# State-space stage: 96 weight units spread evenly over the rounds, outputs ahead of the lag products, x on all partitions

## The reference

```python
sh1, sc1, gt1, sh2, sc2, gt2 = adaln(c, w_mod[layer], b_mod[layer])  # split(silu(c) @ w + b, 6)
csh1, csc1, cgt1, csh2, csc2, cgt2 = adaln(c_ctx, w_mod[layer], b_mod[layer])
h_lat = modulate(rmsnorm(x_lat, norm_mix_pre[layer]), sh1[:, None], sc1[:, None])
h_ctx = modulate(rmsnorm(x_ctx, norm_mix_pre[layer]), csh1, csc1)
# s5_mixer: 128 groups of 16 features, 64 complex states each, for direction in range(2):
    st_ctx = s5_scan(uc_ctx, lam_bar, b_bar, s0, reverse)
    st_lat = s5_scan(uc_lat, lam_bar, b_bar, s_ctx_final, reverse)
    y_lat = y_lat + jnp.einsum('btgp,ghp->btgh', st_lat, c_mat).real
z = jax.nn.gelu(y.reshape(h.shape).astype(h.dtype))
a, g = jnp.split(z @ w_glu, 2, axis=-1)
```

## Time and profile before

| | us |
|---|---|
| median of 3 runs | 3558.69 (3556.96 to 3559.35) |
| the profiled execution, its own time | 3554.54 |
| its span | 3552.7 |
| state-space stage, up to the first GLU matmul | 465.07 |
| TensorE busy over the span | 3286.0 (92%) |
| VectorE, ScalarE, POOL busy | 2145.0, 1380.7, 480.5 |

### The profile page before, as it was taken

One profiled execution on the slowest core, in us unless ns is written; L12 is line 12 of the kernel. 1 busy time (PEld: TensorE's weight loads), 2 busy tenths in 40 slices (PEclk: granted clock), 3 DMA queues, 4 the chain that ended last, 5 costly groups with the idle time before them and its releaser, 6 DMA issues.

```text
span 3552.7 us, 51801 instructions
## 1 busy us (share of the span) xinstructions
PE 3286.0 (92%) x21097; PEld 2763.3 (78%) x21097; DVE 2145.0 (60%) x1850; ACT 1380.7 (39%) x1385; POOL 480.5 (14%) x352
## 2 busy tenths in 40 slices
PE   5788899799999999886789999999999899999998
PEld 3445578688888888675678888888868788888887
DVE  7668755565555555699565555555644555555555
ACT  4446543433333333322234434433323344344332
POOL 2869900000000000096000000000000000000000
PEclk7888899899999999998799999999999999999999
DMA  9988875255555555344145555555524455555552
GB/s 299 305 282 257 260 243 175 91 184 189 185 189 182 190 186 189 107 142 148 36 154 178 186 190 182 186 189 189 177 92 142 142 186 184 187 187 189 189 183 89
DMA packets 351014, 643.22 MB, mean 181 GB/s; under 512 B 21599, under 2 KB 50359, under 8 KB 350519
## 3 DMA queue, kind: packets, MB, share of 16 engines
q1 hardware_dynamic: 309952, 561.68, 48.9%
q10 hardware_dynamic: 40951, 79.98, 6.6%
HBM read 637.54 MB, written 4.06 MB: 181 GB/s over the span
## 4 chain that ended last, share of the span: by engine, by line
PE 83%; DVE 6%; POOL 5%; issue 2%; DMA 2%; ACT 1%; SPq 1%; DVEq 1%; ACTq 0%; POOLq 0%
PE acc L439 49%; PE acc L440 25%; POOL cpow L1841 3%; DMA raw<-in_w_mod_dram 2%; POOL ptmp L1841 1%; PE acc L1263 1%; DVE z L943 1%; DVE w_lo L793 1%; PE acc L1280 1%; PE acc L521 1%; PE acc L533 1%; PE acc L464 1%; PE acc L1188 1%; PE acc L1247 1%; DVE hf L832 0%
## 5 line engine op out<-in xcount | busy, mean ns | idle before, releaser
L439 PE MATMUL acc<-xin,w_hi 128*128 128x512 f32 x5376 | 1915.2, 399 | 58.9 <-DVE xin L807 33.7
L793 DVE TENSOR_TENSOR w_lo<-raw,w_hi 128x2048 fp32r<-128x2048 f32 x484 | 1111.2, 2301 | 1079.0 <-ACT w_hi L640 1078.8
L440 PE MATMUL acc<-xin,w_lo 128*128 128x256 f32 x5376 | 1519.4, 283 | 0.0
L640 ACT ACTIVATE w_hi<-raw 128x2048 fp32r<-128x2048 f32 x484 | 926.8, 1917 | 1365.1 <-PE acc L440 1365.0
L439 PEld LDWEIGHTS acc<-xin,w_hi 128*128 128x128 f32 x5376 | 1017.2, 189 | 312.5 <-issue 35.6
L440 PEld LDWEIGHTS acc<-xin,w_lo 128*128 128x128 f32 x5376 | 1021.5, 190 | 0.0
L439 PE MATMUL acc<-hid,w_hi 128*128 128x512 f32 x2432 | 845.4, 392 | 0.0
L440 PE MATMUL acc<-hid,w_lo 128*128 128x256 f32 x2432 | 681.2, 280 | 0.0
L439 PEld LDWEIGHTS acc<-hid,w_hi 128*128 128x128 f32 x2432 | 455.1, 187 | 101.4
L440 PEld LDWEIGHTS acc<-hid,w_lo 128*128 128x128 f32 x2432 | 459.6, 189 | 0.0
L799 DVE TENSOR_REDUCE tmp<-acc 128x1024 f32<-128x2048 f32 x116 | 265.0, 2284 | 19.9 <-PE acc L440 19.9
(11 more groups left out here) (241 smaller groups left out, 2063.5 us busy)
## 6 DMA issues: line engine op xcount, KB each, us to landing
raw<-in_ffn_w_gate_dram SPq DMA_DIRECT2D x88, 1024.0 KB, 5.2
raw<-in_ffn_w_up_dram SPq DMA_DIRECT2D x88, 1024.0 KB, 5.1
raw<-in_ffn_w_down_dram SPq DMA_DIRECT2D x88, 1024.0 KB, 5.1
raw<-in_w_mod_dram ACTq DMA_DIRECT2D x76, 1024.0 KB, 9.7
raw<-in_w_mlp_in_dram SPq DMA_DIRECT2D x64, 1024.0 KB, 5.2
raw<-in_w_mlp_out_dram SPq DMA_DIRECT2D x64, 1024.0 KB, 5.1
raw<-in_s_w_glu_dram SPq DMA_DIRECT2D x32, 1024.0 KB, 5.3
raw<-in_ab_w_in_dram SPq DMA_DIRECT2D x32, 1024.0 KB, 5.3
```

Of the source, the lines that this page charges most:

```text
L439: pe.matmul(bank, w_hi[:, slot, w], operand[:, kt, :], start=(kt == 0), stop=False)
L440: ins = pe.matmul(bank[:, 0:TOK], w_lo[:, slot, w], operand[:, kt, 0:TOK], start=False, stop=(kt == UK * units - 1))
L640: act.activation(w_hi[:, slot, :], raw[:, slot, :, :].rearrange("p k n -> p (k n)"), ACT.Copy).then_inc(hi_ready, 1)
L793: dve.tensor_tensor(w_lo[:, slot, :], raw[:, slot, :, :].rearrange("p k n -> p (k n)"), w_hi[:, slot, :].bitcast(F32), SUB).then_inc(lo_re ...
```

## The change

Three things. First, weights: `UNIT_OF` lists all 96 units in one order. The first 16 (parts 0 and 1 of MOD) have the old shape, 512 rows by 512 columns in pieces of 2 KB. The other 80 have 256 rows by 1024 columns, so that a piece of a row is 4 KB; they serve two blocks at once. Eight are multiplied ahead of the rounds, then 5 and 6 in turn per round (`FIRST_UNIT`). ScalarE issues them at three places of a round (`ada_load`). Modulation parts 1, 2, 3 are turned at rounds 1, 5, 7.

Second, order: in round k `outputs(k)` now stands ahead of `lag_blocks(k + 1)` and `states(k + 1)`. Lag products go to the lower half of bank 7, so they wait for the copies of the round before (`r_sb`) and `finish` instead of `copy_lam_powers` and `copy_e`. `output_transposes` waits for `r_sb`. VectorE copies the lags inside `powers_of_b`, between its ninth and tenth operation.

Third, x: xs holds all 128 partitions by 4 tokens, loaded in one step; four squares instead of eight, their sums in ss_x, and eight small products with the identity that bring them to the layout of rstd_x.

```diff
-        xs = Region(xin_at, xin_at + 32 * KB)("xs", [64, L // 2, D])
+        xs = Region(xin_at, xin_at + 32 * KB)("xs", [P, L // 2, D])
...
+        xwide = [v.rearrange("(q j) d -> q j d", j=2) for v in (ctx2, x2)]
...
-        MOD = [(0, 1), (2, 3), (6, 8), (10, 12)]
-        ADA = [4, 5, 7, 9, 11] + list(range(13, 24))
-        BLOCK_COL = {MOD[b][v]: (1 - v) * D + b * UN for b in range(4) for v in range(2)}
-        BLOCK_COL.update({m: 2 * D + n * UN for n, m in enumerate(ADA)})
-
-        def ada_units(queue, m, units=range(UK)):
-            col = BLOCK_COL[m]
-            for k in units:
-                if m:
-                    queue.wait_ge(ada_unit, 4 * m + (k - 3))
-                queue.dma_start(raw[:, k, :, :], w_mod[:, k * UK:(k + 1) * UK, col:col + UN]).then_inc(raw_ready[k], 16)
+        def mod_block(b, v):
+            return (1 - v) * D + b * UN, 47 - (16 + 4 * b + 2 * v)
+
+        def ada_block(n):
+            return 2 * D + n * UN, 15 - n
+
+        SINGLE = [mod_block(b, v) for b in range(2) for v in range(2)]
+        PAIRS = [(mod_block(2, v), mod_block(3, v)) for v in range(2)] + [(ada_block(n), ada_block(n + 1)) for n in range(0, KT, 2)]
+        UNIT_OF = [(col, (window,) * 4, [4 * k, 4 * k + 1, 4 * k + 2, 4 * k + 3]) for col, window in SINGLE for k in range(4)]
+        UNIT_OF += [(p[0][0], (p[0][1], p[1][1]) * 2, [2 * j, 2 * j, 2 * j + 1, 2 * j + 1]) for p in PAIRS for j in range(8)]
+        COLUMNS_AT = {1: 1, 5: 2, 7: 3}
+        FIRST_UNIT = [8 + 11 * (r // 2) + 5 * (r % 2) for r in range(KT + 1)]
+        assert FIRST_UNIT[KT] == len(UNIT_OF) == ADA_UNITS
+
+        def ada_load(queue, first, last):
+            for i in range(first, min(last, ADA_UNITS)):
+                slot = i % SLOTS
+                col, _, k = UNIT_OF[i]
+                if i >= SLOTS:
+                    queue.wait_ge(ada_unit, i - 3)
+                if i < 4 * len(SINGLE):
+                    queue.dma_start(raw[:, slot, :, :], w_mod[:, k[0]:k[0] + 4, col:col + UN]).then_inc(raw_ready[slot], 16)
+                else:
+                    queue.dma_start(raw[:, slot, :, :].rearrange("p (k h) n -> p k (h n)", h=2),
+                                    w_mod[:, k[0]:k[0] + 2, col:col + 2 * UN]).then_inc(raw_ready[slot], 16)
...
-            def load_xs(half):
+            def load_xs():
                 for s in range(2):
-                    sp.dma_start(xs[s * NCH:(s + 1) * NCH, :, :], xch[s][:, 4 * half:4 * half + 4, :]).then_inc(xs_in, 16)
+                    sp.dma_start(xs[:, 2 * s:2 * s + 2, :], xwide[s]).then_inc(xs_in, 16)
...
-            load_xs(0)
-            ada_units(sp, 0)
             load_c(0)
+            load_xs()
+            ada_load(sp, 0, 4)
             load_x(0)
-            sp.wait_ge(xs_sq, 4)
-            load_xs(1)
-            ada_units(sp, 1)
-            ada_units(sp, 2)
+            ada_load(sp, 4, 8)
             sp.wait_ge(c_sel, 1)
             load_c(1)
-            ada_units(sp, 3)
             sp.wait_ge(xt_scaled, 1)
             load_x(1)
+            ada_load(sp, 8, 12)
             sp.wait_ge(c_sel, 2)
             load_c(2)
-            ada_units(sp, 4)
             sp.wait_ge(xt_scaled, 2)
             load_x(2)
...
+            def ada_rows(first, last):
+
+                for i in range(first, last):
+                    slot = i % SLOTS
+                    _, window, k = UNIT_OF[i]
+                    pe.wait_ge(raw_ready[slot], 16 * (i // SLOTS + 1))
                     for q in range(UK):
-                        ins = pe.matmul(ps[0][32 * q:32 * q + 32, :], cond[:, kk * UK + q, window:window + 32], raw[:, kk, q, :],
-                                        start=(m + kk == 0), stop=(kk == UK - 1), skip_group_check=True)
+                        ins = pe.matmul(ps[0][32 * q:32 * q + 32, :], cond[:, k[q], window[q]:window[q] + 32], raw[:, slot, q, :],
+                                        start=(i == 0), stop=(i % 4 == 3), skip_group_check=True)
...
-                pe.wait_ge(lpp_sb, min(n + 2, KT))
-                pe.wait_ge(e_sb, 4 * (n + 1))
+                if n == 0:
+                    pe.wait_ge(par_sb, 1)
+                else:
+                    pe.wait_ge(r_sb, n)
+                if n > 1:
+                    pe.wait_ge(z_lo, n - 1)
...
-                            ins = pe.matmul(ps[5][32 * kp:32 * kp + 32, to:to + P],
+                            ins = pe.matmul(ps[7][32 * kp:32 * kp + 32, to:to + P],
...
+                pe.wait_ge(r_sb, min(n + 2, KT))
...
+            pe.wait_ge(b_sb, 3)
+            select_c(0)
+            pe.wait_ge(xs_sq, 4)
+            pe.wait_ge(angle_ready, 1)
+            for f in range(4):
+                for q in range(2):
+                    ins = pe.matmul(ps[2][32 * q:32 * q + 32, 2 * f:2 * f + 2], ident[:, f:P:4], ss_x[:, 2 * q:2 * q + 2], start=True, stop=True)
+            ins.then_inc(ss_tr, 1)
+            ada_rows(0, 8)
...
             for k in range(-1, KT):
-                if k + 1 < KT:
-                    lag_blocks(k + 1, (k + 1) % 2)
-                    states(k + 1, (k + 1) % 2)
+                if k in COLUMNS_AT:
+                    mod_columns(COLUMNS_AT[k])
                 if k >= 0:
                     outputs(k, k % 2)
+                    if k + 1 < KT:
+                        lag_blocks(k + 1, (k + 1) % 2)
                 if k + 1 < KT:
-                    if k in (-1, 2, 4):
-                        pe.wait_ge(ada_sb, {-1: 2, 2: 3, 4: 4}[k])
-                    ada_rows(ADA[k + 1], 15 - (k + 1), (0, 1))
-                if k in (-1, 2, 4):
-                    mod_columns({-1: 1, 2: 2, 4: 3}[k])
+                    states(k + 1, (k + 1) % 2)
+                    if k < 0:
+                        lag_blocks(0, 0)
+                    i0, i1 = FIRST_UNIT[k + 1], FIRST_UNIT[k + 2]
+                if k in COLUMNS_AT:
+                    pe.wait_ge(mod_raw, COLUMNS_AT[k] + 1)
+                if k + 1 < KT:
+                    if k in COLUMNS_AT:
+                        pe.wait_ge(ada_sb, COLUMNS_AT[k] + 1)
+                    ada_rows(i0, i0 + 2)
...
-                    ada_rows(ADA[k + 1], 15 - (k + 1), (2, 3))
+                    ada_rows(i0 + 2, i0 + 4)
                 if k + 2 < KT:
                     transpose_e(k + 2, 1)
-                if 0 <= k < 4:
-                    mod_rows(2 + k // 2, k % 2)
+                if k + 1 < KT:
+                    ada_rows(i0 + 4, i1)
...
-            square_x(0)
             copy_b(2)
             copy_b(3)
+            square_x()
...
-                    ada_units(act, ADA[k + 1] + 1, (0, 1))
+                    i = FIRST_UNIT[k + 1]
+                    ada_load(act, i + 4, i + 6)
                 if k >= 0:
                     copy_output(k)
                 if k + 2 < KT:
                     copy_e(k + 2)
-                    ada_units(act, ADA[k + 1] + 1, (2, 3))
+                    ada_load(act, i + 6, i + 8)
                 if k + 3 < KT:
                     copy_lam_powers(k + 3)
                     normalise_x(k + 3)
-                if 0 <= k < 4:
-                    ada_units(act, ADA[k + 1] + 2)
-                if k in (1, 3):
-                    copy_adarow(2 + k // 2, MOD[2 + k // 2][1])
+                if k + 2 < KT:
+                    ada_load(act, i + 8, FIRST_UNIT[k + 2] + 4)
                 if k == KT - 2:
-                    copy_adarow(4, ADA[KT - 1])
+                    ada_load(act, FIRST_UNIT[k + 1] + 4, FIRST_UNIT[k + 2])
+                if k + 1 in COLUMNS_AT:
+                    copy_adarow(COLUMNS_AT[k + 1], FIRST_UNIT[k + 2])
+                if k == KT - 2:
+                    copy_adarow(4, FIRST_UNIT[KT])
...
+                if between is not None:
+                    between()
                 c(tt(t, pw[1][1], bv[1][0], MUL))
...
+            dve.wait_ge(ss_tr, 1)
+            dve.tensor_scalar(rstd_x[:, :], ps[2][0:64, 0:L], 1.0 / D, EPS, MUL, ADD).then_inc(ss_ready, 1)
             powers_of_b(c0, 0)
-            dve.wait_ge(xs_sq, 8)
-            dve.tensor_scalar(rstd_x[:, :], rstd_x[:, :], 1.0 / D, EPS, MUL, ADD).then_inc(ss_ready, 1)
-            powers([ab[:, 2], ab[:, 3]], uu, L)
             dve.wait_ge(rstd_root, 1)
             dve.reciprocal(rstd_x[:, :], rstd_x[:, :]).then_inc(rstd_ready, 1)
             modulation(cm, 0)
+            powers([ab[:, 2], ab[:, 3]], uu, L)
...
-                if k + 1 < KT:
-                    copy_lags(c0, k + 1)
                 if k:
                     finish(k - 1)
-                if k in (0, 3, 5):
-                    modulation(cm, {0: 1, 3: 2, 5: 3}[k])
                 if k + 2 < KT:
                     dve.wait_ge(s_done, k + 1)
-                    powers_of_b(c0, k + 2)
+                    powers_of_b(c0, k + 2, lambda: copy_lags(c0, k + 1))
+                elif k + 1 < KT:
+                    copy_lags(c0, k + 1)
+                if k in COLUMNS_AT:
```

(1 more changed line is left out.)

49 lines of the change are left out of this document (19 added, 30 removed).

## The result

The changed kernel takes 3575.89 us in the median of 5 runs (3574.53 to 3580.66), the kernel before 3558.69 beside it (3556.96 to 3559.41): 1.005 times as long, with an interval of 1.0038 to 1.0063. The profiled execution took 3574.53 us with a span of 3572.7, against 3554.54 and 3552.7: 20.0 us more. The forecast was 3534.

| stretch | before | after | difference | forecast |
|---|---|---|---|---|
| start, to the lag product of n=2 | 139.56 | 130.65 | -8.9 | -9.5 |
| 13 rounds | 297.2 (22.86 each) | 306.3 (23.56 each) | +9.1 | -16.4 |
| end, to the first GLU matmul | 28.3 | 31.0 | +2.7 | +1 |
| all behind the stage | | | +17.1 | 0 |

What follows compares the result with a forecast made beforehand. Only the state-space stage's 465 us could move, its rounds held by weight loads or POOL's cpow ring. Start -9.5, rounds -16.4, end +1 sum to -24.9 us: 3558.7 becomes 3534 us, range 3510 to 3558.

Steps and rivals of the forecast that it cites:

- Part 1, the start: Up to the third lag product: x loaded whole and fewer units ahead bring the tables earlier, -9.5 us.
- Part 2, the rounds: The 13 rounds between third and sixteenth lag product: 21.6 us each instead of 22.86, -16.4 us.
- DMA sum of 21.1: In each round: the DMA engines' work with evenly spread units, 22.1 us, or 21.1 at a full share of 1.05.
- two rings: In the rounds: DMA work, 21.1 us, and the Toeplitz path from lag product through r, tw, outputs, nearest to 21.8 us.
- 21.8 with tw beside units: In the rounds: the Toeplitz path's length if tw lands beside weight units; 17.4 us at best, 25.5 with both delays.
- columns ahead of outputs: In three rounds: modulation columns turned on TensorE before outputs, a few tenths three times, counted as nothing.
- Rival (d): In the rounds: heavy ones do not wait for weights, so spreading moves nothing; chance left in Rival (b)'s share.
- Rival (b): In the rounds: the Toeplitz path takes both delays, r and tw, 25.5 us a round, 3584 us; chance 0.07.
- TensorE's waits for POOL: In the rounds: outputs no longer wait for cpow, giving 0.8 to 1.6 us against light rounds; POOL's work is 19.3 us.
- Part 3, the end: From the sixteenth lag product to the first GLU matmul: two more units beside tw, +1 us, from 0 to +4.
- Packets of 4 KB: Weight loads throughout: larger packets taken as no gain, with 2 us of one put into the low end.
- the change touches nothing behind it: Behind the state-space stage, after the first GLU matmul at 465.07 us: no change, 0 us.

Runs made afterwards that it cites:

- after_defer: The changed kernel with one wait more: ScalarE issues a round's first two units only when tw of that round has landed; 3599.66 us in one run.
- after_pad32: The changed kernel with 32 unused bytes behind ss_x, so w_hi, w_lo, hid and later tiles lie higher; 3549.07 us, ratio 0.9975.

## Why the prediction was wrong

The profile moved by +20.0 us where -24.9 was forecast. Of these 44.9 us, 25.5 are the rounds', 17.1 stand behind the stage, 1.7 at its end and 0.6 at its start.

**Part 1, the start: right**, -8.9 for -9.5. x over all partitions and the uncovered first table came as worked out, the eighth unit 2 us late (56 for 54); four of VectorE's small operations took 1.26 us, uncontended, where the earlier trace rows had 4.93.

**Part 2, the rounds: wrong**, +9.1 for -16.4, and this is the step that failed: "With the DMA sum of 21.1 I take 21.6 us a round". The step takes the larger of two rings as the length of every round. The DMA sum was right: the work is 20.9 us a round. What the runs showed in place of 21.6 is 23.56 us, with the two rings in turn.

- Five of the seven rounds with five units end on tw and take 23.0 to 25.5 us, 23.9 in the mean, where "21.8 with tw beside units" was priced. r was no dearer than forecast (4.2 us in the median for 5.6 to 6, 3.7 to 7.1 in these rounds); tw was: in these rounds the outputs start 5.9 to 8.2 us after its last issue, where the landing was put at 7.0 beside units, and its median landing from 150 to 400 us is 6.2, where 5 was expected. The outputs take 3.7 to 4.9 us behind their wait, at a granted clock of 0.51 in the round shown, where 2.9 was put.
- The rounds with six units wait 2.2 to 3.3 us for the sixth. The DMA engines do their work at a share of 0.88, not 1.05, by which I divided: between the landing of the units in flight and ScalarE's next issue there is a gap in each of the two rounds looked at, whichever way the round before had ended. The earlier trace rows had 0.87 to 0.97 in rounds that waited for the DMA. 20.9 / 0.88 is 23.7, but the share is no constant: it is 0.89 to 0.92 in the three kernels with the old order.
- "columns ahead of outputs (a few tenths three times, as before elsewhere): nothing" was wrong too. A wait of 1.2 us and 1.9 us of matmuls stand ahead of the outputs in two of the 13 rounds, and these are the two of 27.4 us. The other four rounds with six units take 23.1 in the mean, those with five 22.8, so the unequal number of units costs little.

That a late tw also makes the next units late, as TensorE uses up none meanwhile, is argued and not shown by a run; after_defer, which took the late tw away, held up ScalarE's copies of ew as well.

Nor was it a saving to have the units spread evenly. In the heavy rounds before, the waits for units were 18.6 us over 13 rounds; evenly spread they are 22.1, for seven units more, and with the old order, where the spread is the main thing left in the rounds, the rounds are 22.4 to 22.8 us, as in the kernel before and its layouts (22.4 to 23.0). Rival (d) had the outcome, that spreading moves nothing, and not the reason: the heavy rounds did wait for weights. It had no chance of its own. The text's own sign of being wrong, more than 1 us a round at weight units, was met: 1.7.

**Rival (b)** named the mechanism: lag product behind outputs behind tw makes a ring of the Toeplitz path. Its price of 25.5 us was met to the tenth in the round at 318 us, by luck: r took 6.7 us there, not 9.3, as the forecast had said of x's new place, and tw 8.0 for 7.0 and outputs 4.9 for 2.9 made up for it. As a mean it was too high, since only every second round is of this kind. What neither the forecast nor the rival had is the alternation: a round that ends on tw, then one that ends on a unit.

**TensorE's waits for POOL** went as forecast, from 23.8 us at cpow to 3.1, and gained nothing, for 22.7 us of waits for tw took their place. The two run side by side: the cpow wait was cover for tw. That the sums are so close is chance; after_pad32, with the same stage, has 4.9 for cpow and 31.8 for tw.

**Part 3, the end:** +2.7 for +1, within its bounds of 0 to 4: it has two unit waits, of 3.92 and 2.04 us.

**Packets of 4 KB**: taken at nothing, with 2 us in the low end. The run that undid them, with twice the transfers, was 10 us slower (3 to 17), so nothing is too little, and how much is theirs is open.

**What no part had:** 17 us behind the stage, by "the change touches nothing behind it, so only these 465 us can move". This is the second step that failed, and the 32-byte run of the kernel before shows it. The diff does touch what lies behind, in the line that adds ss_x ahead of `work_at`. With the stage alone, +2.8 us, the kernel would have been no faster and no slower than could be measured.

## What to carry to other kernels

Two rings that use the same DMA engines need not give the larger of their times: price a stage by its DMA work over the share that the trace of before reaches in the rounds that wait for it, and look for what the removed wait was covering. Price what stands behind a new wait at the clock that it will have there: here the outputs went from 2.9 to as much as 4.9 us. Before taking an engine's wait away by moving a step, follow what the step's input waits for: here the old order kept two products between tw and everything behind it. And compare the groups of the untouched code by mean duration first: a few bytes of a new table can move what follows it and change the time of thousands of instructions elsewhere.

## What the hardware showed that was not expected

A pair of 32-bit matmuls (512 and 256 columns) has one of two pitches at a granted clock of 1.00 (2.4 GHz), 346.7 or 353.3 ns, constant over a loop. Unused bytes ahead of the operands' tiles switch it, 32 of them being enough: 3572.44 against some 3557 us. Over all layouts tried it is worth 3523.3 (one run; 3528.7 in the median when repeated) to 3573.2 us, 1.3 to 1.4% of this kernel. The run with both pitches low differs from a run with one of them high by a shift of xin by 64 in place of 192 bytes, though xin is not read in the blocks on hid. Why is not known from these runs.

The stage's own place varied too: between layouts of the kernel before, whose stage is the same program, the first GLU matmul came at 457.9 to 465.4 us. A difference of a few us in one profile of a stage bound by the DMA engines says nothing by itself.
